# A hybrid decoder layer on one core: table tiles loaded a block earlier, bias transfers on another queue

## The reference

```
xn = rmsnorm(x);  q, k, v, gates ... = split(xn @ w_in)
h  = x + W_out( sum over 3 mixers of sigmoid(g_b) * P_b(mixer_b(xn)) )
y  = h + PEER(rmsnorm(h))
```

```
hid = u_tab[expert] . x;   act = gelu(hid) * gate;   out = sum of act * v_tab[expert]
```

## Time and profile before

| | |
|---|---|
| median of 3 runs | 4507.53 us (4501.73 to 4513.12) |
| the profiled execution | 4512.93 us, its span 4511.1 us |
| granted TensorE clock, mean | 0.922 |
| PE busy | 3962.7 us, 88% of the span |
| VectorE, ScalarE, Pool busy | 57%, 27%, 23% |

### The profile page before, as it was taken

The page is one execution under the profiler, slowest core; times in us unless marked ns, Lnnn a source line. Parts: engine busy times, 40 slices in busy tenths (PEclk is TensorE's granted clock), DMA queues, the critical chain, the costliest instruction groups (busy, mean ns, idle before and its releaser), DMA issues. The chain is left out here.

```text
span 4511.1 us, 55275 instructions
## 1 busy us (share of the span) xinstructions
PE 3962.7 (88%) x21975; PEld 3747.5 (83%) x21975; DVE 2576.3 (57%) x4489; ACT 1200.6 (27%) x1885; POOL 1038.6 (23%) x696
## 2 busy tenths in 40 slices
PE   4799884769999699999777777999979999999998
PEld 2698563558888599999777777999979999999998
DVE  3000445342222368687755556666658888888886
ACT  2112334121111222222455554222222221122111
POOL 0001000000000122222344445665542222222221
PEclk8899776589999799999888888999989999999999
DMA  2211110011112012222233335999998887888885
GB/s 98 59 41 36 42 39 19 21 40 43 43 43 74 30 61 78 76 74 80 82 132 119 128 131 193 354 348 345 355 328 278 275 276 261 279 281 274 269 270 188
DMA packets 288525, 694.92 MB, mean 154 GB/s; under 512 B 21745, under 2 KB 135329, under 8 KB 284339
## 3 DMA queue, kind: packets, MB, share of 16 engines
q1 hardware_dynamic: 195675, 370.60, 24.6%
q0 software_dynamic: 73728, 268.47, 16.7%
q10 hardware_dynamic: 18912, 53.04, 3.0%
HBM read 578.38 MB, written 114.16 MB: 154 GB/s over the span
## 5 line engine op out<-in xcount | busy, mean ns | idle before, releaser
L76 PE MATMUL ps<-x_act_high,x_v_high 128*128 128x400 f32 x2048 | 706.6, 345 | 28.8 <-DVE x_v_low L2191 28.8
L77 PE MATMUL ps<-x_act_low,x_v_high 128*128 128x400 f32 x2048 | 703.9, 344 | 0.0
L78 PE MATMUL ps<-x_act_high,x_v_low 128*128 128x400 f32 x2048 | 702.7, 343 | 0.0
L1958 POOL DMA_INDIRECT rows<-in_v,row_of x256 | 244.9, 956 | 757.5 <-DVE xn L1987 725.5
L76 PEld LDWEIGHTS ps<-x_act_high,x_v_high 128*128 128x128 f32 x2048 | 385.8, 188 | 30.0 <-issue 30.0
L1958 POOL DMA_INDIRECT rows<-in_u_rows,row_of x256 | 324.7, 1268 | 372.6 <-DVE row_hid L1984 316.6
L2200 DVE TENSOR_TENSOR xn<-xn,ps 128x400 f32<-128x400 f32 x512 | 290.5, 567 | 175.5 <-PE ps L78 175.4
L77 PEld LDWEIGHTS ps<-x_act_low,x_v_high 128*128 128x128 f32 x2048 | 385.1, 188 | 0.0
L78 PEld LDWEIGHTS ps<-x_act_high,x_v_low 128*128 128x128 f32 x2048 | 384.9, 188 | 0.1
L76 PE MATMUL ps<-hd_high,h_u_high 128*128 128x400 f32 x1024 | 353.9, 346 | 13.7 <-DVE h_u_low L2063 13.7
L1841 PE MATMUL ps<-gm_wgt,gm_hot 128*128 128x128 f32 x1600 | 235.4, 310 | 136.7 <-POOL gm_wgt L1812 136.1
(11 more groups left out here) (342 smaller groups left out, 8017.6 us busy)
## 6 DMA issues: line engine op xcount, KB each, us to landing
x_v_raw<-in_v SPq DMA_DIRECT2D x128, 512.0 KB, 9.8
gates<-gm_out SPq DMA_DIRECT2D x25, 2048.0 KB, 7.2
x_g<-gates SPq DMA_DIRECT2D x32, 1600.0 KB, 10.0
x_act_raw<-kept SPq DMA_DIRECT2D x128, 400.0 KB, 4.9
h_u_raw<-in_u SPq DMA_DIRECT2D x64, 512.0 KB, 7.0
kept<-h_hid ACTq DMA_DIRECT2D x64, 400.0 KB, 6.8
wq_raw<-in_u SPq DMA_DIRECT2D x40, 512.0 KB, 3.5
kept<-kept_act ACTq DMA_DIRECT2D x40, 400.0 KB, 2.4
```

The source lines that it names most:

```text
L76: pe.matmul(out, w[0], x[0], start=first, stop=False)
L77: pe.matmul(out, w[0], x[1], start=False, stop=False)
L78: return pe.matmul(out, w[1], x[0], start=False, stop=last)
L1958: pool.indirect_dma_start(m.rows[:, s % ROWS, :], None, src, bass.IndirectOffsetOnAxis(ap=m.row_of[:, t, k:k + 1], axis=0)).then_inc(r.loa ...
```

## The change

In the projection the skew write and the 16 bias loads leave SP's stream and are issued by Pool, which in this stage does nothing else: it waits for `ext`, issues the skew write, waits for it, issues all 16 loads one behind another and waits for them. In the gate matrix SP issues at the start of block n the tile of block n+2 where it was that of block n+1, and waits first for the split of block n's tile, whose place it takes.

```
             @block.sync
             def _(sp):
-                def load_bias(h):
-                    g = h % 4
-                    src = bass.AP(tensor=d["skew"].tensor, offset=h * P * EXT + P - 1, ap=[[EXT - 1, P], [1, 2 * P]])
-                    sp.dma_start(m.bias[:, h // 4, g, :], src).then_inc(spread, 16)
...
                 for i in range(len(pieces)):
                     if i:
                         sp.wait_ge(low, i)
                     sp.dma_start(raw[:], source(i)).then_inc(loaded, 16)
-                    if i == 1:
-                        sp.wait_ge(ready, 1)
-                        sp.dma_start(d["skew"], ext[:].unsqueeze(1).broadcast_to([8, P, EXT])).then_inc(skewed, 16)
-                    if 8 <= i < 16:
-                        sp.wait_ge(skewed, 16)
-                        load_bias(i - 8)
-                sp.wait_ge(spread, 16 * 16)
                 sp.dma_start(d["out_wvs"][:, 0:WIN - TS, :], d["win_v"][:, TS:WIN, :]).then_inc(m.stored, 16)
+
+            @block.gpsimd
+            def _(pool):
+                pool.wait_ge(ready, 1)
+                pool.dma_start(d["skew"], ext[:].unsqueeze(1).broadcast_to([8, P, EXT])).then_inc(skewed, 16)
+                pool.wait_ge(skewed, 16)
+                for h in range(8):
+                    g = h % 4
+                    src = bass.AP(tensor=d["skew"].tensor, offset=h * P * EXT + P - 1, ap=[[EXT - 1, P], [1, 2 * P]])
+                    pool.dma_start(m.bias[:, h // 4, g, :], src).then_inc(spread, 16)
...
+                pool.wait_ge(spread, 16 * 16)
...
                 for blk in range(TD // TBG):
-                    if 2 <= blk + 1 < BESIDE:
-                        sp.wait_ge(u_low, blk)
-                        sp.dma_start(u_raw[:, (blk + 1) % 2], d["u"][EARLY + blk + 1]).then_inc(u_loaded[(blk + 1) % 2], 16)
+                    if blk + 2 < BESIDE:
+                        sp.wait_ge(u_low, blk + 1)
+                        sp.dma_start(u_raw[:, blk % 2], d["u"][EARLY + blk + 2]).then_inc(u_loaded[blk % 2], 16)
                     sp.wait_ge(copied, 2 * PER * (blk + 1))
                     sp.dma_start(d["gates"][blk], out[:, blk % 2]).then_inc(stored[blk % 2], 16)
```

More of the change, by code:

```diff
@@ L345, in _ @@
             def _(sp):
-                def load_bias(h):
-                    g = h % 4
-                    src = bass.AP(tensor=d["skew"].tensor, offset=h * P * EXT + P - 1, ap=[[EXT - 1, P], [1, 2 * P]])
-                    sp.dma_start(m.bias[:, h // 4, g, :], src).then_inc(spread, 16)
-                    src = bass.AP(tensor=d["skew"].tensor, offset=h * P * EXT + P - 1,
-                                  ap=[[0, NB], [EXT - 1, TS], [1, WK]])
-                    sp.dma_start(m.bias_s[32 * g:32 * g + 32, h // 4, :], src).then_inc(spread, 16)
                 for i in range(len(pieces)):
@@ L357, in _ @@
                     sp.dma_start(raw[:], source(i)).then_inc(loaded, 16)
-                    if i == 1:
-                        sp.wait_ge(ready, 1)
-                        sp.dma_start(d["skew"], ext[:].unsqueeze(1).broadcast_to([8, P, EXT])).then_inc(skewed, 16)
-                    if 8 <= i < 16:
-                        sp.wait_ge(skewed, 16)
-                        load_bias(i - 8)
-                sp.wait_ge(spread, 16 * 16)
-                sp.dma_start(d["out_wvs"][:, 0:WIN - TS, :], d["win_v"][:, TS:WIN, :]).then_inc(m.stored, 16)
+                sp.dma_start(d["out_wvs"][:, 0:WIN - TS, :], d["win_v"][:, TS:WIN, :]).then_inc(m.stored, 16)
+            @block.gpsimd
[7 more added lines that the diff above has]
+                    pool.dma_start(m.bias[:, h // 4, g, :], src).then_inc(spread, 16)
+                    src = bass.AP(tensor=d["skew"].tensor, offset=h * P * EXT + P - 1,
+                                  ap=[[0, NB], [EXT - 1, TS], [1, WK]])
+                    pool.dma_start(m.bias_s[32 * g:32 * g + 32, h // 4, :], src).then_inc(spread, 16)
+                pool.wait_ge(spread, 16 * 16)
             @block.tensor
```

## The result

The changed kernel took 4346.28 us (median of 4 runs, 4343.89 to 4348.38) against 4510.32 us before on the same chip: a ratio of 0.9639, 95% interval 0.9622 to 0.9656, 164 us less. The forecast was 4337 us, 170 less. The profiled execution's span is 4343.2 us, against 4511.1.

The account below looks back on a forecast made before the run. TensorE sets the pace, standing still behind transfers in gate stage and projection. 4512.9 - 161 (tile) - 9 (bias) = 4343, or 4337 us in terms of the median; own range 4325 to 4345, wide range 4312 to 4362 (8 in 10).

Parts of the forecast that it names:

- the prediction's own sign (a landing of 20 us): Projection: a piece taking 20 us to land beside the skew would show that the loads stay behind it.
- rival 1: Projection: loads stay behind the skew on the same engines, so only the gate gain comes, 4347 us; chance 0.20.
- One wait under two names: Gate stage: ScalarE's 108.0 us for the table tile and PE's 136.1 us for Pool's product are one wait.
- Gain per block: Gate stage: a block falls from 24.04 to 16.74 us with 0.86 of PE's wait left; 22 blocks make 161 us.
- Rival 4: Gate stage: the tile did not hold ScalarE; another wait of the same length replaces it, 4499 us; chance 0.03.
- The clock: Gate stage: PE's clock stays up after the short remaining wait, as block 0's 2.02 us group suggested.
- Rival 3: Gate stage: the clock falls in every block after the 0.8 us that remain, 4390 us; chance 0.07.
- What it adds: Gate stage: SP's new wait for the split of the tile two before costs nothing, covered by later waits.
- +3.5 us a load, four loads: Projection: the skew slows each of four loads by 3.5 us, as with h_u_raw; bias part taken as +9 us.
- The rule that spoke against: Projection: issuing engines share the same 16 DMA engines, another saves only sequencer time; the bias part would bring 0.
- Pool's issue: Projection: issuing the skew's 1024 rows takes Pool 7.6 us, 0.8 at the least, hidden because Pool is idle.
- Rival 5: Projection: Pool's transfers end after the stage and its wait for the bias loads makes it slower, 4569 us; chance 0.02.

Follow-up runs that it names:

- e1: Only the table tile loaded a block earlier, bias transfers left on SP's queue, against the kernel before the change: 4351.29 us, ratio 0.9648.
- e5: The full change, but the skew write issued at 108 from ScalarE's queue instead of Pool's: 4338.98 us, one run.

## Why the prediction was right, and where it was not

The total was right because the part that makes nearly all of it was: the table tile, 161 us forecast and 159 measured. The bias part was wrong, and by the prediction's own sign (a landing of 20 us) its rival 1 came true there. The measured 4346 lies at that rival's 4347 and 1 us outside the forecast's own range of 4325 to 4345; the wide range held it because it was drawn to hold rival 1.

- *One wait under two names.* Right. With the tile a block early, ScalarE's 108.0 us and PE's 136.1 went together; e1 shows that this part does it alone.
- *Gain per block.* Forecast 24.04 - 16.74 = 7.30, measured 24.04 - 16.83 = 7.21; times 22 these are 161 and 159. The 0.86 that should stay was 0.71, and the groups around the gap cost some 0.2 more than the free 3.97 each. Rival 4 (another wait takes its place) fell.
- *The clock.* It stayed at 1.00 over the block, as the 2.02 us group of block 0 had said. Rival 3 would have shown as groups of 3.76 in every block; only the stage's first group, behind the 6.6 us, is slow (3.57).
- *What it adds.* SP's new wait and the tile's longer life cost nothing that the rows show; the tile still lands 8.2 us after its issue, and nobody waits for it.
- *The bias part was mis-sized.* The term "+3.5 us a load, four loads" was wrong: the second piece took 21.1 us, the third 6.9 (136.66 to 143.58), the fourth 4.3; the gain was 3.4 us and not 9. I had taken the price from loads beside Pool's gathers, 128 rows each, of which only a few are outstanding (an estimate from their rows: 512 gathers in some 1690 us, 6.8 us each to land, make two at a time). The skew is 1024 rows in one go. The share of 0.46 that I read as room for the loads was room for half of one: that half went at once, the other half stood still for some 9 us and was through about 8 us before the skew was, so it stands behind part of the skew's rows, not all. Moving to Pool also put the skew some 6 us earlier, ahead of the second piece instead of the third, so that most of what the third piece won the second lost. With the skew on Pool but still behind the second piece's load, the third would by these rows have landed some 8 us earlier (29.4 - 21.1, an estimate; this was not run).
- *The rule that spoke against.* The Trainium skill ("DMA: Bandwidth & Descriptors", "Issuing engines are not separate DMA queues") had it nearly so: another queue brought 3.4 us to the projection, and e5 shows the same wait from ScalarE's queue. Beyond the issue time it did bring something: the held load took some 21 us and not 29. The same page ("Queues, rings and completion order") says that an engine goes round its queues packet by packet. The 9 us here in which the second half of a load did not move at all (117 to 126) neither show nor exclude it, since no run shows how long a packet of the skew is.
- *Pool's issue.* 1.27 us for 1024 rows, not 7.6; hidden either way. Rival 5 was far off: the last bias load was issued at 150.7.
- *A slip in the range.* Its gate bound of 168 us should be 170 (161 + 0.43 x 22); nothing hangs on it.

The forecast gain of the whole was 6 us too large. The bias term makes 6 of it and the gate stage 2; differences of untouched stages pulled 2 the other way.

## What to carry to other kernels

When two engines wait in the same stage for about the same time, look for one chain before adding the waits up; the price of the chain is the pace of a stretch of the same trace where its cause is missing (here block 23), and what is left is the next link in the order of the instructions. A transfer that stands in the way is moved in time, into slack, or cut into awaited parts; another queue shortens the wait (here from 29 to 21 us) but does not take the transfer off the engines that carry it. And a moved transfer is also earlier or later than before: ask what it now stands in front of.

## What the runs showed of the hardware that I had not expected

- A 512 KB load beside a write of 1024 rows of 1.5 KB issued before it in one transfer took 18 to 22 us where the write came from another queue (21.1, 21.6, 21.8 from Pool's, 18.0 from ScalarE's) and 28 to 29.5 behind it in SP's own; beside the same write in eight awaited parts at most 4.6.
- That write moved 49 to 52 GB/s from 8 partitions whichever queue issued it, and took Pool a wait of 9.4 us in place of 33 when it went from DRAM to DRAM with an outer count of 128.
- Pool issued a direct transfer of 1024 rows in 1.27 us, little more than the 0.96 us of an indirect gather of 128 rows.
